# Norms of a two-part transformer block kernel: fewer square sums on TensorE, per-block signals, and modulation sums placed before the branches

## What is computed

```python
mod = silu(c) @ ada_w[layer] + ada_b[layer]      # six vectors of 1024
sh1, sc1, g1, sh2, sc2, g2 = split(mod, 6)
h = rms_norm(x, w_mix) * (1 + sc1) + sh1
x = x + g1 * mixer(h)                            # the norm that follows reads this x
h = rms_norm(x, w_ffn) * (1 + sc2) + sh2
x = x + g2 * ffn(h)
```

## Time and profile before

| | |
|---|---|
| median of 3 runs | 2229.43 us |
| lowest and highest run | 2228.62 and 2234.73 us |
| the profiled execution | 2229.48 us |
| its span, first to last instruction | 2227.7 us |
| mean granted TensorE clock | 0.982 |
| PE busy | 2148.6 us, 96% |
| PEld busy | 1931.1 us, 87% |
| DVE busy | 1749.9 us, 79% |
| ACT busy | 1228.6 us, 55% |
| HBM | 575.26 MB read, 259 GB/s over the span |

### The profile page before, as it was taken

How to read it: one execution, slowest core, us unless ns; L and a number is a source line. 1 busy time by engine, 2 the same in 40 slices (tenths; PEclk the granted TensorE clock), 3 DMA queues, 4 the chain that set the end, 5 groups by cost and what they waited for, 6 DMA issues and landing times.

```text
span 2227.7 us, 33379 instructions
## 1 busy us (share of the span) xinstructions
PE 2148.6 (96%) x13865; PEld 1931.1 (87%) x13865; DVE 1749.9 (79%) x1903; ACT 1228.6 (55%) x1367; POOL 54.1 (2%) x101
## 2 busy tenths in 40 slices
PE   6999999999999999999999999999999999999998
PEld 5989999987888888788888888878899998788998
DVE  5998777868899898989999877677776776755665
ACT  3724434736777777677777735541545446324554
POOL 1000000000000000000000000000000000000000
PEclk9999999989999999999999989999999999999999
DMA  9887985638999999999999966537465375234552
GB/s 317 310 321 284 330 295 191 222 138 316 377 379 351 377 373 370 366 373 379 359 372 374 383 212 190 192 130 269 147 195 183 103 223 157 92 130 167 174 184 82
DMA packets 339040, 578.55 MB, mean 260 GB/s; under 512 B 48099, under 2 KB 208955, under 8 KB 326595
## 3 DMA queue, kind: packets, MB, share of 16 engines
q1 hardware_dynamic: 324604, 475.34, 62.4%
q0 software_dynamic: 13824, 100.67, 11.6%
q10 hardware_dynamic: 454, 0.34, 0.1%
HBM read 575.26 MB, written 1.05 MB: 259 GB/s over the span
## 4 chain that ended last, share of the span: by engine, by line
PE 81%; DVE 10%; ACT 4%; DMA 2%; issue 2%; SPq 1%; DVEq 0%; ACTq 0%; POOL 0%; POOLq 0%
PE bank L597 80%; ACT arena L1569 2%; DVE w_low L2114 2%; DVE ada_acc L2122 2%; DVE arena L2122 1%; DMA ada_in<-in_ada_w 1%; DVE arena L2114 1%; SPq L497 1%; PE bank L1328 1%; DMA ring<-in_moe_w 1%; DVE arena L2608 1%; ACT L1569 1%; DVE h L2122 1%; DVE x L2122 0%; ACT mix_hi L1569 0%
## 5 line engine op out<-in xcount | busy, mean ns | idle before, releaser
L2114 DVE TENSOR_TENSOR w_low<-ring,moe_w_hi 128x2048 fp32r<-128x2048 f32 x264 | 594.5, 2284 | 13.9 <-ACT moe_w_hi L1569 9.9
L1569 ACT ACTIVATE moe_w_hi<-ring 128x2048 fp32r<-128x2048 f32 x264 | 506.4, 1919 | 172.8 <-DMA ring<-in_moe_w 133.9
L597 PE MATMUL bank<-h_hi,w_hi 128*128 128x256 f32 x1056 | 263.2, 287 | 10.8 <-ACT h_hi L1569 5.8
L597 PE MATMUL bank<-h_hi,w_low 128*128 128x256 f32 x1056 | 262.4, 285 | 0.0
L597 PE MATMUL bank<-mix_h_hi,mix_hi 128*128 128x256 f32 x800 | 235.2, 297 | 15.3 <-DVE w_low L2114 7.8
L597 PE MATMUL bank<-mix_h_hi,w_low 128*128 128x256 f32 (+2 forms) x848 | 242.1, 288 | 0.0
L597 PE MATMUL bank<-h_low,mix_hi 128*128 128x256 f32 x800 | 216.3, 286 | 0.0
L597 PEld LDWEIGHTS bank<-h_hi,w_hi 128*128 128x128 f32 x1056 | 202.7, 192 | 13.2 <-issue 6.9
L2122 DVE SCALAR_TENSOR_TENSOR ada_acc<-ada_in,c_col,ada_acc 128x2048 f32<-128x2048 f32 x84 | 197.3, 2348 | 15.5 <-DMA ada_in<-in_ada_w 10.5
L597 PEld LDWEIGHTS bank<-h_hi,w_low 128*128 128x128 f32 x1056 | 204.0, 193 | 0.0
L1569 ACT ACTIVATE arena<-bank 128x512 f32<-128x512 f32 (+2 forms) x171 | 90.1, 527 | 199.2 <-PE bank L597 195.8
(11 more groups left out here) (219 smaller groups left out, 4573.4 us busy)
## 6 DMA issues: line engine op xcount, KB each, us to landing
ring<-in_moe_w SPq DMA_DIRECT2D x264, 1024.0 KB, 6.7
ada_in<-in_ada_w POOLq DMA_DIRECT2D x96, 1024.0 KB, 7.5
ring<-in_w_in SPq DMA_DIRECT2D x56, 1024.0 KB, 5.6
ring<-in_ffn_w_up SPq DMA_DIRECT2D x44, 1024.0 KB, 7.8
ring<-in_ffn_w SPq DMA_DIRECT2D x33, 1024.0 KB, 8.0
ring<-in_ffn_w_down SPq DMA_DIRECT2D x22, 1024.0 KB, 4.9
ring<-in_w_out SPq DMA_DIRECT2D x16, 1024.0 KB, 5.3
ring<-in_w_br_mla SPq DMA_DIRECT2D x4, 1024.0 KB, 5.0
```

Of the source, the lines that this page charges most:

```text
L597: ins = nc.tensor.matmul(out, lhsT, rhs, start=start, stop=stop, skip_group_check=shared)
L1569: return nc.scalar.activation(out, in_, f, **kw)
L2114: return nc.vector.tensor_tensor(out, a, b, op)
```

## The change

`residual` no longer waits and signals by pairs: each update of a block signals `x_ready` itself, and the four banks are freed together at the end. `squares` takes the last pair in two steps of one block. Behind the four mixers VectorE adds the squares of blocks 2 and 3 and then of 4 and 5 onto those of 0 and 1 (`add_squares`), before it waits for the last bank, and TensorE sums four blocks: 0, 1, 6 and 7. The norms behind the feed-forward blocks keep eight sums, with the new signals. The modulation sums of the columns `4 * KB` to `5 * KB` move: in mixer1 of layer 1 from behind `norm_sum` to between the halves of `wout`, in both mixer2 from behind `wout2` to before the branches, each with VectorE's steps for them.

```diff
+SQUARE_STEPS = ((0, 2), (2, 2), (4, 2), (6, 1), (7, 1))
 # TensorE
-            def norm_sum():
+            def norm_sum(added=False):
                 fill(1)
                 sq = region(0, KB * T).rearrange("p (k t) -> p k t", k=KB)
-                for kb in range(KB):
-                    if kb % 2 == 0:
-                        need("norm_sq")
+                ready = {0: 4, 6: 1, 7: 1} if added else dict.fromkeys((kb for kb, _ in SQUARE_STEPS), 1)
+                for kb in (0, 1, 6, 7) if added else range(KB):
+                    if kb in ready:
+                        need("norm_sq", ready[kb])
                     mm(bank[1][:, 0:T], ones, sq[:, kb, :], start=(kb == 0), stop=(kb == KB - 1),
                        inc="norm_sum" if kb == KB - 1 else None)
...
             def conv_ffn_norm():
-                fill(6)
-                modulation(6, 4 * KB, 5 * KB)
-                norm_sum()
+                norm_sum(added=True)
                 fill(2)
                 modulation(2, 5 * KB, MODS)
                 keep_busy(2)
...
                 if li == 0:
                     need("ada_done")
-                    fill(0)
-                    modulation(0, 2 * KB, 4 * KB)
+                fill(0)
+                modulation(0, *((2 * KB, 4 * KB) if li == 0 else (4 * KB, 5 * KB)))
                 for j, b in enumerate(banks):
...
+                if li:
+                    need("ada_done")
+                fill(1)
+                modulation(1, 4 * KB, 5 * KB)
                 need("yla_sb", 4)
...
             mixer1(0)
-            norm_sum()
+            norm_sum(added=True)
...
             mixer1(1)
-            norm_sum()
-            ffn_modulation()
+            norm_sum(added=True)
+            fill(6)
+            modulation(6, 5 * KB, MODS)
+            keep_busy(2, 7)
             moe_route()
 # ScalarE
             def squares():
-                for j in range(KB // 2):
-                    need("x_ready", 2)
-                    func(region(j * 2 * T, 2 * T), x[:, 2 * j:2 * j + 2, :].rearrange("p k t -> p (k t)"),
+                for k, n in SQUARE_STEPS:
+                    need("x_ready", n)
+                    func(region(k * T, n * T), x[:, k:k + n, :].rearrange("p k t -> p (k t)"),
                          ACT.Square).then_inc(s["norm_sq"], 1)
 # VectorE
                 if li == 0:
                     late(li, 4)
                     modulation(0, 2 * KB, 4 * KB, 0)
+                else:
+                    modulation(1, 4 * KB, 5 * KB, 0)
...
-            def residual(banks, gate_col, name, beside=None):
+            def residual(norms, banks, gate_col, name, beside=None):
                 for j, b in enumerate(banks):
                     if beside:
                         beside(j)
+                    if j == 3 and norms % 2:
+                        add_squares(5 + 11 * (norms // 2))
                     need(name)
                     for i in range(2):
                         k = 2 * j + i
-                        ins = stt(x[:, k, :], bank[b][:, i * T:(i + 1) * T], mod[:, gate_col + k:gate_col + k + 1],
-                                  x[:, k, :], ALU.mult, ALU.add)
-                    settle(ins)
+                        stt(x[:, k, :], bank[b][:, i * T:(i + 1) * T], mod[:, gate_col + k:gate_col + k + 1],
+                            x[:, k, :], ALU.mult, ALU.add).then_inc(s["x_ready"], 1)
+                dve.wait_ge(s["x_ready"], (norms + 1) * KB)
+                for b in banks:
                     dve.sem_inc(bank_free[b], 1)
-                    dve.sem_inc(s["x_ready"], 2)
+
+            def add_squares(earlier):
+                total = region(0, 2 * T)
+                dve.wait_ge(s["norm_sq"], earlier + 2)
+                settle(tt(total, total, region(2 * T, 2 * T), ALU.add))
+                dve.wait_ge(s["norm_sq"], earlier + 3)
+                tt(total, total, region(4 * T, 2 * T), ALU.add).then_inc(s["norm_sq"], 1)
...
                 gated_attention(0, 0)
                 gated_attention(1, 7)
+                modulation(2 + li, 4 * KB, 5 * KB, 1)
                 gated_heads(1)
...
-                residual((0, 5, 3, 7), 16, "wout_psum", lambda j: ada_next((2, 2, 2, 1)[j]))
+                residual(5 + 2 * li, (0, 5, 3, 7), 16, "wout_psum", lambda j: ada_next((2, 2, 2, 1)[j]))
                 if li == 0:
                     ada_finish(3, 2)
-                modulation(2 + li, 4 * KB, 5 * KB, 6)
...
             mixer1(1)
-            norm(scale_a[:, 1, :], h, "norm_mul", columns=(1, 4 * KB, 5 * KB, 7))
-            modulation(1, 5 * KB, MODS, 0)
+            norm(scale_a[:, 1, :], h, "norm_mul")
+            modulation(1, 5 * KB, MODS, 6)
             moe_route()
```

More of the change, by code:

```diff
@@ L1521, in _ @@
             mixer2(1)
-            need("ada_done")
             conv_ffn_norm()
@@ L2419, in beside @@
                         split_low("w", 0, 0, (j - 1,))
-                residual((2, 3, 4, 5), 16, "wout_psum", beside)
+                residual(1 + 2 * li, (2, 3, 4, 5), 16, "wout_psum", beside)
                 late(li, 1, 0)
@@ L2674, in ffn @@
                 low(("rgx", 1, 0))
-                residual((4, 5, 6, 7), 40, "down_part")
+                residual(2, (4, 5, 6, 7), 40, "down_part")
                 dve.sem_inc(s["down_done"], 1)
@@ L2886, in conv_ffn @@
                     low(("kr", 1, 0))
-                residual((4, 5, 6, 7), 40, "down_part")
+                residual(6 + 2 * li, (4, 5, 6, 7), 40, "down_part")
                 dve.sem_inc(s["down_done"], 1)
```

## The result

The changed kernel is slower. Its median of 13 runs is 2235.48 us (2230.24 to 2239.59), that of the kernel before, run beside it, 2228.15 us (2220.94 to 2234.73). The ratio is 1.003, with a 95% interval from 1.0018 to 1.0042. The difference is 7.3 us, where -0.25 us was forecast; the time lies outside the range, and the difference is past the 6.7 us (0.3%) that the prediction said the measurement can tell.

What follows compares the result with a forecast made beforehand. The chain ending last was taken as mostly TensorE (PE 81% of the span), touched at seven norms. Terms +0.8, -0.9, +0.6, about +2.4, -0.95 and -2.2 gave -0.25 us from 2229.43: 2229.2 us, range 2223.5 to 2234.5.

Steps and rivals of the forecast that it cites:

- Norm 8: Last norm of the kernel: ScalarE is busy throughout, so nothing was counted.
- Norm 1: Behind mixer1 of layer 0: adds delay the last pair, +0.5 us, and the clock costs +0.3, together +0.8 us.
- The third rival: Low clock lasts past the product at norm 1, and norm 5's fall joins the existing one: 2236.2 us, chance 0.07.
- The first: Rival: the clock holds in TensorE's new holes at norms 1 and 5, 1.9 us less: 2227.3 us, chance 0.15.
- the second rival: The 1.2 GHz stretch before norm 7's feed-forward block disappears as well: 2224 us, or 2222, chance 0.11.
- Norm 5: Behind the first mixer2: moved sums +1.1, late last pair +1.25, fewer sums -1.5, clock +1.6: about +2.4 us.
- Norms 3 and 7: Behind mixer1 of layer 1 and the second mixer2: adds hidden in VectorE's waits; +0.6 us and -2.2 us in all.
- fifth rival: At norm 7 the last square or its signal binds, not the sums: 3.3 us come back, 2232.5 us, chance 0.07.
- The moved sums of mixer2: Modulation sums before the branches: 1.89 us less TensorE's 0.81 us wait, so +1.1 us each; bounds 0 and 1.9.
- Norms 2 and 6: Behind the dense and first convolution block: eight VectorE updates without waits take 3.26 us, not 4.24; -0.9 and -0.95 us.
- fourth rival: Removing VectorE's waits gives nothing at norms 2 and 6: +1.85 us, 2231.0 us, chance 0.10.
- shift the rest one for one: Whole kernel: any shift of a norm moves everything behind it equally, as nothing there has its own start.

Runs made afterwards that it cites:

- the fastest kernel: Changed kernel with bank 4 of the last residual freed early, adds only at norms 3 and 7, mixer1's modulation sums back behind `norm_sum`: 2220.73 us, ratio 0.997.
- the early bank: Changed kernel, but behind the last residual VectorE frees bank 4 after its first pair, as the kernel before did: 2229.88 us, ratio 0.9996.

## Why the prediction was wrong, point by point

**Norm 8 is the step that failed.** The prediction said: "At norm 8 ScalarE is busy throughout; I count nothing." That was read from the kernel before and was true there; the prediction put the term at nothing and looked no further. It costed what the change takes from VectorE, the waits and signals by pairs, and not what these pairs also did: free a bank each. The diff in front said that the four banks are freed together at the end, and the question that was not put is who takes a freed bank first. At norm 8 it is TensorE, with the first sums of its final code. The stall of 1.42 us is the smaller part of the 4.54 us that ScalarE then waits; the larger is work at 0.50. Size: 4.8 us in the trace (3.8 in the fastest kernel). By the ratios it is 0.34%, 7.6 us, between the changed kernel with and without the early bank, and 0.13%, not clear of noise, in the fastest one; why the first is more than its stage is open. In all six profiles with the late bank the clock fell 0.6 to 2.3 us behind the last update; in the three pairs of kernels that differ by the bank alone (the changed one, the one before, the fastest) the last norm takes 3.8 to 6.1 us more with it.

**Norm 1: right mechanism, wrong size.** The adds were to delay the last pair by 0.5 us and the clock to cost 0.3 us, since "the table load and the product cover most of it". They cover the square sums, but neither the modulation sums behind them nor the start of the dense block. In all five profiles with the adds and no filling the clock fell, for 6.8 to 13.7 us; in none of the two with filling; and without adds it fell in two of the seven, for 6.8 us each. The five stages are 2.1 to 4.0 us longer than before, for a term of +0.8. The own part of it, +0.5 in the forecast, came to 0.5 with the clock held by filling (209.1 against 208.6), though not where it was put: the last pair starts only 0.1 us later (8.22 against 8.11). So it is the clock's +0.3 that failed: 1.6 to 3.5 us. The price stands in the earlier trace rows; what was mis-sized was how long the low clock lasts, and that it reaches through the modulation sums into the block.

**The third rival** had this as its mechanism, with a chance of 0.07, at 2236.2 us, 0.7 us from the median. It is half right: in two of the five profiles with adds TensorE was at 0.50 when the product ended, as the rival asked, in the others the clock fell later and still cost 1.6 us or more. The closeness of its figure is partly luck, since the last norm, which it does not have, made up more than half of the loss.

**The first and the second rival.** The first, that the clock holds in the new holes, fell: it was at 0.50 in the sums of norm 5 and around norm 1. The second came half true: the stretch at 0.50 before norm 7's block lasted 3.4 us in both profiles in place of 6.8, and from norm 7's products to norm 8's first pair it took 198.4 and 198.3 us in place of 199.5.

**Norm 5** came out as predicted in the two profiles of after: +1.35 us without the moved sums, measured +1.24 and +1.36. Behind it there were two stretches at 0.50, of 3.4 us each, where the kernel before has one. The kernels without adds and with filling at norm 1 have the same code at norm 5, and there it took 24.2 and 25.1 us. The adds themselves are no gain there: 23.8 us with them, 20.8 without.

```profile
1565.34 0.87 DVE L2128 SCALAR_TENSOR_TENSOR x<-bank,mod,x 128x256 f32<-128x256 f32 x2
1565.57 3.37 PE L599 MATMUL bank<-arena,const 128*128 128x256 f32 x8 [3.18 <-DVE arena L2120]
...
1568.97 0.39 ACT L1575 ACTIVATE arena<-bank 128x256 f32<-128x256 f32 x1 [2.31 <-PE bank L599]
```
```profile
1557.21 0.87 DVE L2130 SCALAR_TENSOR_TENSOR x<-bank,mod,x 128x256 f32<-128x256 f32 x2
...
1559.36 0.38 ACT L1577 ACTIVATE arena<-bank 128x256 f32<-128x256 f32 x1 [0.83 <-PE bank L601]
```

These are after, and the kernel with adds at norms 3 and 7 alone. Four sums at 0.50 take 3.37 us (3.5 forecast); eight sums at 1.00, most of them done before the last pair, let the root follow that pair after 2.15 us in place of 3.63.

**Norms 3 and 7.** Norm 3: forecast +0.6, measured +0.43; the moved sums make its last pair 1.8 us later (1.9 forecast), and what VectorE is late by at the first pair, 3.1 us, it catches up in its waits, as foretold. At norm 7 the root was to come 1.9 us behind the last pair and -3.3 us; it comes after 2.16 us, -3.16 us, so the fifth rival fell:

```profile
2016.72 0.88 DVE L2128 SCALAR_TENSOR_TENSOR x<-bank,mod,x 128x256 f32<-128x256 f32 x2 [4.57 <-PE bank L599]
...
2018.88 0.38 ACT L1575 ACTIVATE arena<-bank 128x256 f32<-128x256 f32 x1 [0.83 <-PE bank L599]
```

At norm 3 the root stands right behind the table load, as foretold:

```profile
480.70 1.28 ACT L1575 ACT_TABLE_LOAD   x1
482.00 0.38 ACT L1575 ACTIVATE arena<-bank 128x256 f32<-128x256 f32 x1
```

**The moved sums of mixer2** were taken at +1.1 us each. Ahead of norm 7 they cost 0.2 to 0.7 us: 218.7 and 218.9 us without them, 219.0 to 219.4 in eight profiles with them. In four profiles this stage has one more stretch at 0.50, of 3.4 us near its start; then it took 219.8 (the kernel before) and 220.1 us without them and 220.9 and 221.0 with them, about 1 us more. Ahead of norm 5 nothing shows (230.7 to 232.0 us in ten profiles with them, 230.4 to 233.1 in four without).

**Norms 2 and 6** were to give 0.9 and 0.95 us, and gave 0.82 and 0.80. The eight updates now stand in one row, before:

```profile
1769.43 3.23 DVE L2128 SCALAR_TENSOR_TENSOR x<-bank,mod,x 128x256 f32<-128x256 f32 x8 [1.05 <-PE bank L599]
```

The fourth rival fell: the waits of 0.24 us between pairs did cost, and 4.24 us became 3.23. The signals themselves cost next to nothing: eight updates with one each take 3.23 us, and eight operations of the same form at norm 4, with one signal behind the last, take 3.21 (at 1315.36 us before, at 1325.02 us after). The Trainium skill, in "VectorE: DVE Perf Modes", section "The DRAIN you can't avoid", says of a semaphore after each copy that it costs nothing extra. The trace agrees for the signals; a wait on one's own last result between two instructions is another matter, as the 0.24 us show.

**Together.** Predicted for norms 1 to 7: -0.25 us. With norm 1 as measured (+3.6 in place of +0.8) and the rest as the stages show, they come to about 0, and the last norm adds 4.8. That is 4.7 us by the stages of the first profile and 5.1 by the second, against 7.3 us between the medians. The two or three microseconds between are within what stages with the same code differ by, and no run settles them. The prediction took these stages as fixed ("shift the rest one for one"); they added 5.4 us in the first profile and 1.6 in the second. Two slips in its working, 459.3 for 459.2 and +2.4 for +2.45, change nothing.

## What to carry to other kernels

When a release (a bank, a buffer, a signal) moves to a later place, list for each instance of the code who takes it next, the last one above all, where the code behind it is another. Time taken from the critical engine's work in a hole is not a gain if its clock falls for it: price a new hole by the work that follows it, not by its own length. At norm 1 the low clock lasted 7 to 14 us and cost 1.6 to 3.5 us. And an add on another engine that replaces sums is worth it only where that engine waits anyway (norms 3 and 7 here), which the trace of before shows.

## What the runs showed of the hardware that was not expected

The granted clock fell behind shorter waits than the 2.88 us before norm 7. At the end of the changed kernel TensorE waited 1.90 us and, 4.5 us later, 1.42 us before sums of a single column; the first of these waits is in every kernel, and the clock fell 1.0 us behind the last update, where it fell 4.0 us behind it in the kernel before, with TensorE's work done. It stayed at 0.50 for all the 8.7 us of work that were left. The second wait is not needed for a fall: in two of the eight profiles with bank 4 freed early the clock also fell about 2 us behind the last update, with most of the sums done, and the last norm took 13.8 and 13.9 us in place of 13.3 to 13.4.

The Trainium skill, in "TensorE: Matmul & The Clock Gate", section "Part 1: The HAM clock gate", says that activity releases the throttle. The traces do not bear this out for every kind of work: TensorE was busy for all of those 8.7 us without getting the clock back, and at norm 1 for all 10.1 us before it did.

The fall is not the same in each execution of one kernel: the two profiles of after differ by 1.45 us from norm 1's last pair to its first product (6.69 and 8.14 us), and of the seven profiles without adds at norm 1 two had a fall there and five had none. What decides it in the single case stays open.

Matmuls whose result nobody reads paid for themselves in the stages: norm 1 209.1 and 209.4 us with them, 210.7 to 212.6 with adds and without filling. In the kernel's time that does not show: the ratios of the two kernels with the early bank and all adds, 0.9991 filled and 0.9996 not, can't be told apart.
